# Seven row slots instead of nine, four weight tiles held in their place, and the choice of experts cut into four parts

## The chip, the cores and the metric

The kernel runs on one core of a Trainium2 chip. The core has five engines with a program each: TensorE (PE, with its weight loads as PEld), VectorE (DVE), ScalarE (ACT), GpSimd (POOL) and SyncE (SP), and 16 DMA engines that all transfers share. The metric is the device time of one execution in microseconds (us). Before the change it was 1616.74 us, the median of 3 runs (1616.18 to 1619.26).

## The reference, cut to what matters

Two layers over 256 positions of width 1024. Each has a token mixer (a gated MLP in the first, gated linear attention in the second), then a PEER block. All is float32; every sum below is what the kernel computes.

```
for i in range(2):
    h = rmsnorm(x, norm_mix[i]);  x = x + mixer_a(...) if i == 0 else x + mixer_b(...)
    h = rmsnorm(x, norm_ffn[i]);  x = x + peer(h, ...)
return rmsnorm(x, final_norm)

def peer(h, w_q, k1, k2, u_tab, v_tab):          # per position, 8 heads
    q = h @ w_q                                   # 8 x 256
    s1, s2 = q[:128] . k1, q[128:] . k2           # 128 scores each
    v1, i1 = top_k(s1, 16);  v2, i2 = top_k(s2, 16)
    top_s, pos = top_k(v1 + v2 (all 256 pairs), 16)
    eid  = i1 * 128 + i2 at pos                   # expert numbers, 16 per head
    gate = softmax(top_s)
    act  = gelu(u_tab[eid] . h)                   # 16 dots of length 1024
    return sum over heads and picks of gate * act * v_tab[eid]

mixer_b: proj = h @ w_in; decays, chunked attention; o = rmsnorm(o) * silu(r); return o @ w_out
```

## The kernel before

The 256 positions are two halves (h = 0, 1) of 128, one position per partition. A *row* n is one pick of one head for one half: its GpSimd gather fetches for each of the 128 positions the 2048 numbers (u and v) of that position's expert, 128 x 8 KB = 1.05 MB, into one of 9 row slots (`ROW_SLOTS`, `gather`, L407). There are 2 layers x 2 halves x 8 heads x 16 picks = 512 rows; 16 rows of one head are a *group* j, and k is the row's place in it. Row n passes through every engine:

- VectorE: `dot` (L944) multiplies the u half with hn and sums it, when the gather has landed.
- ScalarE: `gelu` for a pair of rows (L573, `BATCH` = 2), and `weigh` (L587), which makes a diagonal matrix of gate x gelu.
- TensorE: the diagonal times the v half, two products of 512 columns (each two instructions), accumulated in PSUM; it then raises `row_used` (L1399).
- GpSimd: the gather of row n + 9 waits for `row_used` of row n. The first of a group, k = 0, also waits for `ids_ready`, the group's expert numbers.

The numbers of group j come from `choose(j)` on VectorE (L890): two lists of 128 scores cut to 16 each, 112 candidate sums cut to 16, then positions turned into numbers. It stands as one piece behind dot k = 7 of the group before (L1082), for j = 16 and 24 behind k = 1 (`NEXT_CHOICE`). `gates` (L937) stands behind k = 13 and waits for ScalarE's exponentials.

Every engine's order is the order in which its program is written; nothing is reordered. Beside the rows, tables of numbers (`SUMS`, `FIRST_QK`, `FIRST_RV`, `FIRST_BOUT`, `HEAD_PLACES` and so on) say behind which row each step of other work stands: the first layer's queries during rows 0 to 39, the second mixer for half 0 during rows 128 to 255 and for half 1 during rows 256 to 383, the second layer's queries in between and after.

Weights of that other work are tiles of 128 x 1024 (0.5 MB) which SyncE loads through 4 `raw` slots in the order of the list `WEIGHTS` (L102), each when TensorE has used the tile 4 places before (`weight_used`). The second mixer's output weights `b_out`, 8 tiles, stand there twice, once for each half. `block_row` (L1252) uses them.

The row slots are laid over the memory that the first mixer used, the second mixer's tensors (`gq` and so on) behind them.

Of the kernel before, what the change touches and what calls it, by code (L numbers as in the profile page):

```python
# [29 lines left out]
F32 = mybir.dt.float32  # L30
# [7 lines left out]
P = 128  # L38
D = 1024
# [3 lines left out]
TILE = 1024  # L43
# [16 lines left out]
P_HEADS = 8  # L60
P_ROWS = 2 * P_HEADS
NK = 128
TOPK = 16
PICKS = P_HEADS * TOPK
ROWS = TT * PICKS
GROUPS = 2 * TT * P_HEADS
# [8 lines left out]
ROW_SLOTS = 9  # L75
# [16 lines left out]
N_WQ = P_ROWS  # L92
# [10 lines left out]
    [("b_qk", c, 0) for c in range(N_BQK)] + [("b_rv", c, 0) for c in range(N_BRV)] + [("b_out", c, 0) for c in range(N_BOUT)]  # L103
# [4 lines left out]
    + [("b_out", c, 1) for c in range(N_BOUT)] + [("w_q1", c, 1) for c in range(N_WQ)])  # L108
# [9 lines left out]
NEXT_CHOICE = 113  # L118
# [39 lines left out]
def trunk(nc, t, out):  # L158

    with ExitStack() as ctx:  # L160
# [3 lines left out]
        def sem(name):  # L164
            return ctx.enter_context(nc.semaphore(name))
# [9 lines left out]
        def overlay(parts):  # L175
# [46 lines left out]
            ("pad_rows", [P, ROW_SLOTS * 2 * D], F32),  # L222
# [16 lines left out]
        ])  # L239
        ed, qe, ke = [ed0, ed1], [qe0, qe1], [ke0, ke1]  # L240
# [51 lines left out]
        early_loaded = sem("early_loaded")  # L292
# [35 lines left out]
        def _(sp):  # L328
# [4 lines left out]
            def load(src, slot):  # L333
                sp.dma_start(raw[slot][:, :], src).then_inc(raw_loaded[slot], 16)
# [28 lines left out]
            for m, (name, c, h) in enumerate(WEIGHTS):  # L363
                if m < RAW_SLOTS:
                    sp.wait_ge(query_used, N_WQ - RAW_SLOTS + m + 3)
                else:
                    sp.wait_ge(weight_used, m - RAW_SLOTS + 1)
                load(t[name][c], m % RAW_SLOTS)
            for b in range(2 * TT):
                h, cols = b // 2, slice(b % 2 * BANK, b % 2 * BANK + BANK)  # L370
                sp.wait_ge(hn_ready[4], b + 1)
                sp.dma_start(out[h][:, cols], hn[:, h, cols]).then_inc(stored, 16)
# [352 lines left out]
        def _(dve):  # L725
# [18 lines left out]
            def after(number):  # L744
                dve.wait_ge(dve_chain, number)
# [144 lines left out]
            def choose(j):  # L890
# [4 lines left out]
                else:  # L895
# [3 lines left out]
                      [topi[:, h, k, :] for k in range(2)])  # L899
                after(chain[0])  # L900
# [7 lines left out]
                after(d1)  # L908
                top16([cand[:, h, :]], [candv[:, h, :]], [candpos[:, h, :]])
# [16 lines left out]
                after(d2)  # L926
                full = [P, 2, TOPK, TOPK]
# [69 lines left out]
            def mix(h, w):  # L997
# [52 lines left out]
                if w == NEXT_CHOICE:  # L1050
                    choose((2 + h) * P_HEADS)
# [13 lines left out]
            choose(0)  # L1065
            for n in range(2 * ROWS):
                dot(n)
                _, h, g, k = group_of(n)
                w = n % PICKS
                j = n // TOPK + 1  # L1070
                if n == 1:
                    gates(0)
                if PICKS <= n < 3 * PICKS:
                    mix(n // PICKS - 1, w)
                if n >= 3 * PICKS:
                    if w == SUMS:
                        add_sums(4, 0, 4, [(row_used, 3 * PICKS)] * 2)
                    if w == ROOT:
                        add_eps(4, 0)
                    if w == SCALED:  # L1080
                        scale(4, 0, 3)
                if k == TOPK // 2 - 1 and j < GROUPS and j not in (2 * P_HEADS, 3 * P_HEADS):  # L1082
                    choose(j)
                if k == TOPK - 3 and j < GROUPS:
                    gates(j)
# [8 lines left out]
        def _(pe):  # L1094
# [157 lines left out]
            def block_row(name, c, h, a, bank, start, stop):  # L1252

                w = weight(name, c, h)
                for d in range(2):
                    ins = product(psum[:, bank + d, :], a, w[:, d * BANK:(d + 1) * BANK], start=start, stop=stop)
                ins.then_inc(weight_used, 1)
# [207 lines left out]
```

## Time and profile before

| | |
|---|---|
| median of 3 runs | 1616.74 us |
| the profiled execution, its time | 1616.94 us |
| its span | 1614.9 us |
| TensorE busy, share of the span | 1379.0 us, 85% |
| VectorE | 1040.0 us, 64% |
| ScalarE | 661.1 us, 41% |
| GpSimd | 588.6 us, 36% |
| mean granted TensorE clock | 0.952 |
| moved by DMA | 632.15 MB, mean 391 GB/s |

The span is from the first to the last instruction on the core; the time has a little around it. Busy shares of engines overlap, since they work side by side, and are averages over stages that have different limits: the first mixer until about 180 us, the rows afterwards. The granted clock is the share of 2.4 GHz that TensorE got.

### The profile page before, as it was taken

How to read it: one execution, taken by the hardware profiler on the slowest of the kernel's cores; microseconds unless marked ns; L12 is line 12 of the kernel's file. 1: busy time of each engine (PE TensorE's matmuls, PEld its weight loads, DVE VectorE, ACT ScalarE, POOL GpSimd, SP SyncE). 2: the span in 40 equal slices, each digit the busy share in tenths (PEclk: the TensorE clock that was granted, in tenths of full speed). 3: DMA queues.
4: the chain of work that ended last, by engine and by line, in shares of the span. 5: the costliest groups of instructions: out<-in, count | busy, mean ns of one | idle time of the engine just before them, and what ended most of it. 6: DMA issues, size and time to landing. Idle time of an engine off the chain costs nothing. (4 is left out here: it accounts for less than half of the span.)

```text
span 1614.9 us, 15347 instructions
## 1 busy us (share of the span) xinstructions
PE 1379.0 (85%) x4384; PEld 742.2 (46%) x4384; DVE 1040.0 (64%) x2628; ACT 661.1 (41%) x1731; POOL 588.6 (36%) x536
## 2 busy tenths in 40 slices
PE   7998899977777799997968899899988788887776
PEld 6877756522333364443334565345334344443332
DVE  4684566666666666767666655786566566666664
ACT  4653333333333445744333355553343433333333
POOL 0100244443444433334434334243434334444442
PEclk9999999999999899998999999899999999899999
DMA  6855599999999999999999999999999999999997
GB/s 245 298 206 190 214 422 418 423 417 421 419 419 419 409 414 422 421 423 401 424 418 421 421 422 423 409 423 422 421 422 393 422 422 417 422 404 421 416 408 300
DMA packets 99634, 632.15 MB, mean 391 GB/s; under 512 B 11168, under 2 KB 11296, under 8 KB 33504
## 3 DMA queue, kind: packets, MB, share of 16 engines
q0 software_dynamic: 75504, 545.01, 81.7%
q1 hardware_dynamic: 24048, 86.19, 14.0%
q8 instruction: 34, 0.56, 0.1%
q14 instruction: 48, 0.39, 0.1%
HBM read 630.10 MB, written 1.05 MB: 391 GB/s over the span
## 5 line engine op out<-in xcount | busy, mean ns | idle before, releaser
L1096 PE MATMUL psum<-row,diag 128*128 128x512 f32 x2048 | 973.6, 622 | 212.3 <-ACT diag L594 210.9
L415 POOL DMA_INDIRECT row<-in_uv,ids x512 | 576.8, 1127 | 937.3 <-PE psum L1096 721.7
L950 DVE SCALAR_TENSOR_TENSOR row<-row,hn 128x1024 f32<-128x1024 f32 x512 | 617.0, 1224 | 400.9 <-DMA row<-in_uv,ids 393.3
L1096 PEld LDWEIGHTS psum<-row,diag 128*128 128x128 f32 x2048 | 390.0, 198 | 712.9 <-issue 411.7
L576 ACT ACTIVATE acted<-dots 128x2 f32<-128x2 f32 (+1 forms) x257 | 52.1, 203 | 707.5 <-DVE row L950 706.9
L594 ACT ACTIVATE diag<-gate_diag,acted 128x128 f32<-128x128 f32 x512 | 177.9, 387 | 0.2
L585 ACT ACTIVATE gate_diag<-consts,gate 128x128 f32<-128x128 f32 x512 | 173.8, 386 | 0.0
L730 DVE TENSOR_TENSOR tile_lo<-raw,tile_hi 128x1024 fp32r<-128x1024 f32 x48 | 58.7, 1223 | 58.8 <-ACT tile_hi L446 58.8
L1096 PE MATMUL psum<-raw,hT_mix 128*128 128x512 f32 x192 | 90.2, 592 | 0.0
L446 ACT ACTIVATE tile_hi<-raw 128x1024 fp32r<-128x1024 f32 x48 | 50.7, 1058 | 76.7 <-PE psum L1096 72.6
L1096 PEld LDWEIGHTS psum<-hT_query,raw 128*128 128x128 f32 x512 | 63.1, 194 | 15.4 <-issue 15.4
L1096 PE MATMUL psum<-hT_query,raw 128*128 128x128 f32 x512 | 63.0, 277 | 0.0
L1096 PEld LDWEIGHTS psum<-raw,hT_mix 128*128 128x128 f32 x192 | 36.5, 190 | 45.9 <-issue 45.9
L950 DVE DVE_READ_ACCUMULATOR row<-row,hn 128x1 f32 x512 | 42.1, 82 | 0.0
L569 ACT ACT_TABLE_LOAD x32 | 41.1, 1283 | 0.6
L568 ACT ACT_TABLE_LOAD x31 | 39.8, 1283 | 0.6
L940 DVE TENSOR_REDUCE head_sum<-gate 128x1 f32<-128x16 f32 x32 | 5.4, 168 | 46.5 <-ACT gate L568 46.1
L1096 PE MATMUL psum<-tile_hi,hT_hi 128*128 128x512 f32 x128 | 34.7, 393 | 0.5 <-ACT hT_hi L481 0.5
L1096 PE MATMUL psum<-tile_hi,hT_lo 128*128 128x512 f32 x128 | 34.3, 390 | 0.7 <-DVE hT_lo L779 0.7
L1096 PEld LDWEIGHTS psum<-hT_mix,raw 128*128 128x128 f32 x256 | 31.0, 192 | 7.2 <-issue 7.2
L1096 PE MATMUL psum<-tile_lo,hT_hi 128*128 128x512 f32 x128 | 34.2, 389 | 0.0
L576 ACT ACT_TABLE_LOAD x25 | 32.1, 1283 | 0.5
(184 smaller groups left out, 1033.9 us busy)
## 6 DMA issues: line engine op xcount, KB each, us to landing
raw<-in_w_q SPq DMA_DIRECT2D x40, 512.0 KB
raw<-in_a_in SPq DMA_DIRECT2D x32, 512.0 KB
raw<-in_b_rv SPq DMA_DIRECT2D x32, 512.0 KB
raw<-in_a_out SPq DMA_DIRECT2D x16, 512.0 KB
row<-in_uv,ids POOLq DMA_INDIRECT x512
raw<-in_b_qk SPq DMA_DIRECT2D x16, 512.0 KB
raw<-in_b_out SPq DMA_DIRECT2D x16, 512.0 KB
early_q<-in_w_q SPq DMA_DIRECT2D x8, 512.0 KB, 5.8
```

Of the source, the lines that this page charges most:

```text
L415: pool.indirect_dma_start(rows[s][:, :], None, t[f"uv{l}"][:, :], bass.IndirectOffsetOnAxis(ids[:, h, g, k:k + 1], 0)).then_inc(row_loaded ...
L446: act.activation(tile_hi[slot % SPLIT_SLOTS][:, :], raw[slot][:, :], ACT.Copy).then_inc(hi_ready, 1)
L568: act.activation(gate[:, h, g, :], gate[:, h, g, :], ACT.Exp).then_inc(exps, 1)
L569: act.preload_act_table(ACT.Gelu)
L576: act.activation(acted[:, h, g, k:k + many], dots[:, h, g, k:k + many], ACT.Gelu).then_inc(gelu_done, 1)
L585: act.activation(gate_diag[:, n % (2 * BATCH), :], ident, ACT.Copy, scale=gate[:, h, g, k:k + 1]).then_inc(gate_spread, 1)
L594: act.activation(diag[:, n % DIAGS, :], gate_diag[:, n % (2 * BATCH), :], ACT.Copy, scale=acted[:, h, g, k:k + 1]).then_inc(diag_ready, 1)
L730: dve.tensor_tensor(tile_lo[s][:, :], raw[slot][:, :], tile_hi[s][:, :].bitcast(F32), ALU.subtract).then_inc(lo_ready, 1)
L940: after(did(dve.tensor_reduce(head_sum[:, h:h + 1], gate[:, h, g, :], AX.X, ALU.add)))
L950: dve.scalar_tensor_tensor(u, u, 1.0, hn[:, h, :], ALU.mult, ALU.mult, accum_out=dots[:, h, g, k:k + 1]).then_inc(dotted, 1)
L1096: return pe.matmul(o, a, b, start=start, stop=stop, skip_group_check=True)
```

## The change

Three things. `ROW_SLOTS` goes from 9 to 7, and in the memory of the two slots lie four tiles `held0` to `held3`, loaded once with the first four tiles of `b_out` (between the loads of `b_rv` for half 0) and used for both halves; the list `WEIGHTS` has `b_out` from tile 4 on only. `choose` becomes a generator with three stops, so four parts, and one part stands behind each of the dots k = 4 to 7 (behind k = 0 to 3 for j = 16 and 24). `NEXT_CHOICE` goes.

```diff
--- before.py
+++ after.py
@@ -72,7 +72,8 @@
 NARROW = 4
 CANDS = WIDE_ROWS * TOPK + (TOPK - WIDE_ROWS) * NARROW
 
-ROW_SLOTS = 9
+ROW_SLOTS = 7
+HELD = 4
 BATCH = 2
 DIAGS = 8
 FIRST_Q = 6
@@ -100,12 +101,12 @@
 HEADS_AHEAD = 2
 HEADS_EARLY = 6
 WEIGHTS = (
-    [("b_qk", c, 0) for c in range(N_BQK)] + [("b_rv", c, 0) for c in range(N_BRV)] + [("b_out", c, 0) for c in range(N_BOUT)]
+    [("b_qk", c, 0) for c in range(N_BQK)] + [("b_rv", c, 0) for c in range(N_BRV)] + [("b_out", c, 0) for c in range(HELD, N_BOUT)]
     + [("w_q1", c, 0) for c in range(2 * HEADS_EARLY)][:2 * HEADS_AHEAD]
     + [("w_q1", c, 0) for c in range(2 * HEADS_AHEAD, 2 * HEADS_EARLY)]
     + [("b_qk", c, 1) for c in range(N_BQK)] + [("b_rv", c, 1) for c in range(N_BRV)]
     + [("w_q1", c, 0) for c in range(2 * HEADS_EARLY, N_WQ)]
-    + [("b_out", c, 1) for c in range(N_BOUT)] + [("w_q1", c, 1) for c in range(N_WQ)])
+    + [("b_out", c, 1) for c in range(HELD, N_BOUT)] + [("w_q1", c, 1) for c in range(N_WQ)])
 PLACE = {w: m for m, w in enumerate(WEIGHTS)}
 
 
@@ -115,7 +116,7 @@
 FIRST_RV, SIGMOID, SILU = 29, 48, 51
 OUT, O_SCALED, O_TURN, FIRST_BOUT = 65, 73, 73, 77
 X_SUMS, X_ROOT, X_TURN = 95, 97, 100
-NEXT_CHOICE = 113
+FIRST_PART = 4
 HEAD_PLACES = (
     [(0, g, PICKS + 104 + 6 * g) for g in range(2)] + [(0, 2 + i, 2 * PICKS + 3 * i) for i in range(4)]
     + [(0, 6 + i, 2 * PICKS + 62 + 8 * i) for i in range(2)]
@@ -219,7 +220,7 @@
             ("b_in", [P, 2 * A_WIDTH], F32),
         ])
         (_, gq, gk, gcum, ed0, ed1, qe0, qe1, ke0, ke1, k_last, score_in, score_x, bv, br, bo, masks) = overlay([
-            ("pad_rows", [P, ROW_SLOTS * 2 * D], F32),
+            ("pad_rows", [P, 18 * TILE], F32),
             ("gq", [P, B_HEADS, P], F32),
             ("gk", [P, B_HEADS, P], F32),
             ("gcum", [P, B_HEADS, P], F32),
@@ -237,6 +238,7 @@
             ("bo", [P, D], F32),
             ("masks", [P, B_LEVELS + 1, P], U32),
         ])
+        held = overlay([("pad_slots", [P, ROW_SLOTS * 2 * D], F32)] + [(f"held{j}", [P, TILE], F32) for j in range(HELD)])[1:]
         ed, qe, ke = [ed0, ed1], [qe0, qe1], [ke0, ke1]
         z_la, z_tmp = qe0.rearrange("p a b -> p (a b)"), ke0.rearrange("p a b -> p (a b)")
         early_b = overlay([("pad_early", [P, 21 * TILE], F32)] + [(f"early_q{j}", [P, TILE], F32) for j in range(EARLY_Q // 2)])[1:]
@@ -289,7 +291,7 @@
         ain_biased, ain_gelu = sem("ain_biased"), sem("ain_gelu")
         v_meaned, v_squares, v_ms, v_std, v_normed = sem("v_meaned"), sem("v_squares"), sem("v_ms"), sem("v_std"), sem("v_normed")
         sv_done, y_ready, y_turned, yT_hi_ready, yT_lo_ready = sem("sv_done"), sem("y_ready"), sem("y_turned"), sem("yT_hi_ready"), sem("yT_lo_ready")
-        early_loaded = sem("early_loaded")
+        early_loaded, held_loaded = sem("early_loaded"), sem("held_loaded")
         gates_ready, gate_spread, ids_ready, shifted, exps = (
             sem("gates_ready"), sem("gate_spread"), sem("ids_ready"), sem("shifted"), sem("exps"))
         query_used = sem("query_used")
@@ -366,6 +368,8 @@
                 else:
                     sp.wait_ge(weight_used, m - RAW_SLOTS + 1)
                 load(t[name][c], m % RAW_SLOTS)
+                if N_BQK <= m < N_BQK + HELD:
+                    sp.dma_start(held[m - N_BQK][:, :], t["b_out"][m - N_BQK]).then_inc(held_loaded, 16)
             for b in range(2 * TT):
                 h, cols = b // 2, slice(b % 2 * BANK, b % 2 * BANK + BANK)
                 sp.wait_ge(hn_ready[4], b + 1)
@@ -897,6 +901,7 @@
                 after(chain[0])
                 top16([scores[:, h, 2 * g + k, :] for k in range(2)], [topv[:, h, k, :] for k in range(2)],
                       [topi[:, h, k, :] for k in range(2)])
+                yield
                 after(chain[0])
                 for ranks, cols, place in ((slice(0, WIDE_ROWS), slice(0, TOPK), slice(0, WIDE_ROWS * TOPK)),
                                            (slice(WIDE_ROWS, TOPK), slice(0, NARROW), slice(WIDE_ROWS * TOPK, CANDS))):
@@ -906,6 +911,7 @@
                     did(dve.tensor_tensor(cand[:, h, place].rearrange("p (a b) -> p a b", a=m), v1, v2, ALU.add))
                 d1 = did(dve.tensor_copy(topi16[:, h, :, :], topi[:, h, :, :]))
                 after(d1)
+                yield
                 top16([cand[:, h, :]], [candv[:, h, :]], [candpos[:, h, :]])
                 after(chain[0])
                 dve.tensor_tensor(gate[:, h, g, :], candv[:, h, :], candv[:, h, 0:1].broadcast_to([P, TOPK]),
@@ -924,6 +930,7 @@
                 after(d2)
                 d2 = did(dve.tensor_tensor(pos[:, h, 1, :], pos[:, h, 1, :], part2[:, h, :], ALU.add))
                 after(d2)
+                yield
                 full = [P, 2, TOPK, TOPK]
                 d2 = did(dve.tensor_tensor(look[:, 0:2, :, :], pos[:, h, :, :].unsqueeze(3).broadcast_to(full),
                                            iota[:, 0:TOPK].unsqueeze(1).unsqueeze(1).broadcast_to(full), ALU.is_equal))
@@ -1047,8 +1054,6 @@
                     add_eps(3, h)
                 if w == X_TURN:
                     scale(3, h, 2)
-                if w == NEXT_CHOICE:
-                    choose((2 + h) * P_HEADS)
 
             for h in range(TT):
                 add_sums(1, h, 2 * h, [(sums_done, 2 * h + 1), (sums_done, 2 * h + 2)])
@@ -1062,7 +1067,9 @@
                 dve.wait_ge(hn_turned[1], 3 + half)
                 dve.tensor_copy(hT[:, 4 * half:4 * half + 4, P:T],
                                 psum[:, 6 + half, :].rearrange("p (a b) -> p a b", a=4)).then_inc(hT_ready, 1)
-            choose(0)
+            for _ in choose(0):
+                pass
+            choice = iter(())
             for n in range(2 * ROWS):
                 dot(n)
                 _, h, g, k = group_of(n)
@@ -1079,8 +1086,10 @@
                         add_eps(4, 0)
                     if w == SCALED:
                         scale(4, 0, 3)
-                if k == TOPK // 2 - 1 and j < GROUPS and j not in (2 * P_HEADS, 3 * P_HEADS):
-                    choose(j)
+                if j < GROUPS and k == (FIRST_PART if j % P_HEADS or j == P_HEADS else 0):
+                    choice = choose(j)
+                if k < FIRST_PART + 4:
+                    next(choice, None)
                 if k == TOPK - 3 and j < GROUPS:
                     gates(j)
             add_sums(4, 1, 6, [(last_row_half, 1), (row_used, 2 * ROWS)])
@@ -1251,10 +1260,14 @@
 
             def block_row(name, c, h, a, bank, start, stop):
 
-                w = weight(name, c, h)
+                kept = name == "b_out" and c < HELD
+                w = held[c] if kept else weight(name, c, h)
+                if kept:
+                    pe.wait_ge(held_loaded, 16 * HELD)
                 for d in range(2):
                     ins = product(psum[:, bank + d, :], a, w[:, d * BANK:(d + 1) * BANK], start=start, stop=stop)
-                ins.then_inc(weight_used, 1)
+                if not kept:
+                    ins.then_inc(weight_used, 1)
 
             def head_query(h, g, part):
 
```

VectorE's instructions at one choice of the first layer, before: `row,dots` is a dot, `topv` and `topi` are the 16 best of a list of scores and their places, `cand` the 112 sums, `candv` and `candpos` their 16 best.

```order
L950 SCALAR_TENSOR_TENSOR row,dots<-row,hn 128x1024 x10
L876 MAX topv<-scores 128x8 x2
L879 MAX_INDEX topi<-topv,scores 128x8 x2
L882 MATCH_REPLACE scores<-topv,scores 128x128 x2
L885 MAX topv<-scores 128x8 x2
L888 MAX_INDEX topi<-topv,scores 128x8 x2
L906 TENSOR_TENSOR cand<-topv 128x64
L906 TENSOR_TENSOR cand<-topv 128x48
L907 CAST topi<-topi 128x32
L876 MAX candv<-cand 128x8
L879 MAX_INDEX candpos<-candv,cand 128x8
L882 MATCH_REPLACE cand<-candv,cand 128x112
```

The same place in the changed kernel:

```order
L957 SCALAR_TENSOR_TENSOR row,dots<-row,hn 128x1024 x7
L880 MAX topv<-scores 128x8 x2
L883 MAX_INDEX topi<-topv,scores 128x8 x2
L886 MATCH_REPLACE scores<-topv,scores 128x128 x2
L889 MAX topv<-scores 128x8 x2
L892 MAX_INDEX topi<-topv,scores 128x8 x2
L957 SCALAR_TENSOR_TENSOR row,dots<-row,hn 128x1024
L911 TENSOR_TENSOR cand<-topv 128x64
L911 TENSOR_TENSOR cand<-topv 128x48
L912 CAST topi<-topi 128x32
L957 SCALAR_TENSOR_TENSOR row,dots<-row,hn 128x1024
L880 MAX candv<-cand 128x8
```

The choice now begins behind 7 dots of the run, not 10; a dot stands between the scores' best and the sums, and one between the sums and their best.

The end of a choice on VectorE, before (`look` and `numbers` turn positions into expert numbers, `ids`; `head_sum` is the first of the gates):

```order
L925 TENSOR_TENSOR pos<-pos,part 128x16
L928 TENSOR_TENSOR look<-pos,consts 128x512
L931 TENSOR_TENSOR look<-look,topi 128x512
L933 TENSOR_REDUCE numbers<-look 128x32
L935 SCALAR_TENSOR_TENSOR ids<-numbers 128x16
L950 SCALAR_TENSOR_TENSOR row,dots<-row,hn 128x1024 x6
L940 TENSOR_REDUCE head_sum<-gate 128x1
```

And changed:

```order
L931 TENSOR_TENSOR pos<-pos,part 128x16
L957 SCALAR_TENSOR_TENSOR row,dots<-row,hn 128x1024
L935 TENSOR_TENSOR look<-pos,consts 128x512
L938 TENSOR_TENSOR look<-look,topi 128x512
L940 TENSOR_REDUCE numbers<-look 128x32
L942 SCALAR_TENSOR_TENSOR ids<-numbers 128x16
L957 SCALAR_TENSOR_TENSOR row,dots<-row,hn 128x1024 x6
L947 TENSOR_REDUCE head_sum<-gate 128x1
```

A dot stands ahead of the last part too; the six dots between the choice and the gates stay.

SyncE's loads from the second mixer's half 0 on, before (`raw` the four slots that rotate):

```order
L334 DMA raw<-in_b_qk 128x1024 x8
L334 DMA raw<-in_b_rv 128x1024 x16
L334 DMA raw<-in_b_out 128x1024 x8
L334 DMA raw<-in_w_q 128x1024 x12
L334 DMA raw<-in_b_qk 128x1024 x8
L334 DMA raw<-in_b_rv 128x1024 x16
L334 DMA raw<-in_w_q 128x1024 x4
L334 DMA raw<-in_b_out 128x1024 x8
L334 DMA raw<-in_w_q 128x1024 x16
```

And changed, `held` the four tiles that stay:

```order
L336 DMA raw<-in_b_rv 128x1024
L372 DMA held<-in_b_out 128x1024
L336 DMA raw<-in_b_rv 128x1024 x12
L336 DMA raw<-in_b_out 128x1024 x4
L336 DMA raw<-in_w_q 128x1024 x12
L336 DMA raw<-in_b_qk 128x1024 x8
L336 DMA raw<-in_b_rv 128x1024 x16
L336 DMA raw<-in_w_q 128x1024 x4
L336 DMA raw<-in_b_out 128x1024 x4
L336 DMA raw<-in_w_q 128x1024 x16
```

Four loads of `b_out` stand in each half instead of eight; the piece begins just ahead of the fourth held one, and the first three stand in the same way before it.

## Rows read from the trace of the kernel before

**Rows 1.** The page: span, the DMA engines in 40 slices, the gathers' queue.
```profile
span 1614.9 us, 15347 instructions
...
DMA  6855599999999999999999999999999999999997
...
q0 software_dynamic: 75504, 545.01, 81.7%
```

**Rows 2.** Stretches: PE, PEld, DVE, ACT, POOL busy (x count), PEclk, DMA share, GB/s.
```profile
200.00:1600.00 1400.00, 1193.61 (x3519) 592.48 (x3518) 919.36 (x2441) 565.11 (x1595) 573.56 (x513) 0.95 1.01 418
200.00:330.00 130.00, 128.35 (x407) 73.99 (x406) 83.81 (x225) 49.05 (x150) 58.43 (x51) 0.99 1.01 421
380.00:400.00 20.00, 12.16 (x25) 5.21 (x25) 17.05 (x59) 8.27 (x23) 6.93 (x6) 0.83 1.02 421
540.00:1300.00 760.00, 664.81 (x2138) 339.89 (x2136) 502.78 (x1344) 338.80 (x892) 293.98 (x261) 0.96 1.01 418
600.00:740.00 140.00, 126.06 (x367) 61.71 (x365) 96.89 (x252) 74.62 (x167) 53.12 (x47) 0.97 1.02 422
1220.00:1240.00 20.00, 19.15 (x85) 11.58 (x84) 11.88 (x49) 8.00 (x22) 8.52 (x8) 0.98 0.93 363
```

**Rows 3.** Who waited for whom: GpSimd; total us, times, longest.
```profile
POOL row L415 <- PE psum L1096: 721.7, 442, 8.2
POOL row L415 <- DVE ids L935: 193.7, 22, 113.4
```

**Rows 4.** Timeline, two steady rows and a choice: start, duration, engine, line, idle before.
```profile
366.62 1.23 DVE L950 SCALAR_TENSOR_TENSOR row<-row,hn 128x1024 f32<-128x1024 f32 x1 [1.26 <-DMA row<-in_uv,ids]
...
369.12 1.23 DVE L950 SCALAR_TENSOR_TENSOR row<-row,hn 128x1024 f32<-128x1024 f32 x1 [1.26 <-DMA row<-in_uv,ids]
...
371.52 3.70 PE L1096 MATMUL psum<-row,diag 128*128 128x512 f32 x8 [1.29 <-ACT diag L594]
...
373.77 0.94 POOL L415 DMA_INDIRECT row<-in_uv,ids  x1 [2.34 <-PE psum L1096]
...
375.49 0.94 POOL L415 DMA_INDIRECT row<-in_uv,ids  x1 [0.78 <-PE psum L1096]
...
380.19 0.48 DVE L876 MAX8 topv<-scores 128x8 f32<-128x128 f32 x2
...
382.66 0.34 DVE L906 TENSOR_TENSOR cand<-topv 128x64 f32<-128x64 f32 x2
...
383.13 0.28 DVE L876 MAX8 candv<-cand 128x8 f32<-128x112 f32 x1
...
386.18 0.69 DVE L928 TENSOR_TENSOR look<-pos,consts 128x512 bf16<-128x512 bf16 x1
...
388.17 1.22 DVE L950 SCALAR_TENSOR_TENSOR row<-row,hn 128x1024 f32<-128x1024 f32 x1
388.52 1.68 POOL L415 DMA_INDIRECT row<-in_uv,ids  x1 [3.88 <-DVE ids L935]
...
389.31 1.22 DVE L950 SCALAR_TENSOR_TENSOR row<-row,hn 128x1024 f32<-128x1024 f32 x1
...
391.71 8.71 PE L1096 MATMUL psum<-row,diag 128*128 128x512 f32 x16 [6.57 <-ACT diag L594]
```

**Rows 5.** Timeline: the first gather, and the first dot.
```profile
183.96 1.00 POOL L415 DMA_INDIRECT row<-in_uv,ids  x1 [113.41 <-DVE ids L935]
...
190.66 1.23 DVE L950 SCALAR_TENSOR_TENSOR row<-row,hn 128x1024 f32<-128x1024 f32 x1 [7.00 <-DMA row<-in_uv,ids]
```

**Rows 6.** Timeline in the query stage: gather 33 and dot 31, counted from 0.
```profile
268.38 0.96 POOL L415 DMA_INDIRECT row<-in_uv,ids  x1 [2.01 <-PE psum L1096]
...
270.10 1.25 DVE L950 SCALAR_TENSOR_TENSOR row<-row,hn 128x1024 f32<-128x1024 f32 x1
```

**Rows 7.** Timeline beside the second mixer, group 22: a query copy, and its gates.
```profile
1222.80 0.28 ACT L556 ACTIVATE qT<-psum 128x128 f32<-128x128 f32 x1 [3.15 <-PE psum L1096]
...
1228.14 0.17 DVE L940 TENSOR_REDUCE head_sum<-gate 128x1 f32<-128x16 f32 x1 [7.55 <-ACT gate L568]
```

## The prediction

> **What bounds the kernel now.** I read the page first, then stretches, then waits, then the timeline at the places where the change acts. The page shows the 16 DMA engines over 90% busy from the sixth slice to the last but one, and the gathers' queue with 82% of their time [rows 1]. The stretches put a number on it: wherever the queue is full the engines move 422 GB/s, over 600 to 740 us for instance, with TensorE busy 126 of 140 us; over 200 to 1600 us the mean is 418 [rows 2]. So nearly the whole program runs at the rate of the transfers, and what it loses to them is 1400 x (1 - 418/422) = 13.3 us. Of that, 540 to 1300 us (where the second mixer and the second layer's queries run beside the gathers) has 760 x 4/422 = 7.2 us, the query stage 200 to 330 us has 130 x 1/422 = 0.3 us, and the rest, steady gathering, 5.8 us [rows 2]. One execution counts: its time was 1616.9 us for a span of 1614.9, within 0.2 us of the median of the three runs shown.
>
> The losses come in bursts. The clearest is 1220 to 1240 us, 363 GB/s [rows 2]. The waits say what starves the queue: GpSimd waits for TensorE to free a slot (442 times, which costs nothing while the queue is full), and 22 times for expert numbers from VectorE; without the first of 113.4 us that is 80.3 us over 21 times, 3.8 us each [rows 3]. The timeline shows one: the choice holds VectorE from 380.19 to 388.17 us, 7.98 us, and GpSimd, with a free slot, sits 3.88 us until the numbers are there; TensorE then idles 6.57 us and runs its next 16 matmuls in 8.71 us where 8 took 3.70, at a mean clock of 0.83 in that stretch [rows 2, 4].
>
> **Part 1, four tiles held.** Eight loads of b_out for half 0 and eight for half 1 become eight and four: four loads of 128 x 1024 x 4 B = 0.52 MB less, 2.10 MB. At 422 GB/s [rows 2] that is 5.0 us off a queue that sets the time. The held loads move earlier, between loads of b_rv; the engines serve them at the same price, so the move is worth 0, and if they delay gathers then, they free as much time later. The extra wait of TensorE on them is for loads issued some 50 rows earlier: 0.
> The row gives 422 GB/s. The page "DMA: Bandwidth & Descriptors" of the Trainium skill, section "Where 436 GB/s comes from", says that for HBM to SBUF the HBM side (about 358 GB/s per core) binds; by it the 2.10 MB would be worth 5.9 us. This case's trace does not agree, at 422, and I use 422.
>
> **Part 2, the choice in four parts.** It has the same instructions, so VectorE's total stays. From the timeline the parts last 2.47 us (from 380.19 to the sums at 382.66), 0.47 (to 383.13), 3.05 (to 386.18) and 1.99 us (to 388.17) [rows 4]. A dot takes 1.15 us back to back (388.17 to 389.31), a row comes every 2.48 us (366.62 to 369.12) [rows 4]. So behind dot 4 the next starts 1.15 + 2.47 - 2.48 = 1.1 us late, then 0.3 late behind the second part, 0.3 + 1.15 + 3.05 - 2.48 = 2.0 late behind the third, 2.6 behind the fourth, 1.3 a row later, 0 two later. ScalarE takes dots in pairs, so what counts is the odd row of a pair: at most 2.0 us late. Now it is the whole 7.98 us less one row's slack of 1.33, 6.6 us. The wait for expert numbers goes: with seven slots gather 16j waits for row 16j-7, the tenth row of its group, and the numbers are ready after the eighth. What is late next is only the slot.
>
> **Part 3, seven slots.** A slot's round, from rows: from the start of the even dot (366.62) through TensorE (371.52) to the end of the next gather's issue in its slot (373.77 + 0.94) is 8.1 us; for the odd one 376.43 - 369.12 = 7.3 us [rows 4]. From the end of an issue to the dot, with nothing queued ahead, the one observation is the first gather: 190.66 - 184.96 = 5.7 us [rows 5]. Together 13.8 and 13.0 us. Seven slots at 2.48 us give 17.4, spare 3.6 us; nine give 22.4, spare 8.6. Now 6.6 us of lateness, plus the 3.8 us wait, exceeds 8.6 by a little: this is the loss of 5.8 us over some fifteen steady groups, 0.4 each. Afterwards 2.0 of lateness stands against 3.6: no loss. I leave 1 us for it (bounds 0 and 5.8).
> The row says 5.7 us for a gather alone. The same page of the skill, section "Anatomy of one DMA — SWDGE (gpsimd) path", has a fixed 2.0 us and the bytes at 436 GB/s, which for 1.05 MB would be 4.4 us; the spare would be 4.9 us and not 3.6. It leaves the sum as it is.
>
> The price of fewer slots shows where TensorE is the limit. In the query stage it is busy 128.35 of 130 us [rows 2]: it falls behind the gathers row by row, and nine slots let the transfers run on. With two fewer, gather 31 can't be issued before gather 33 is now, at 269.34 us, since it waits for the same row; with 5.7 us its dot starts at 275.0 instead of 270.10 [rows 5, 6]. TensorE's own times don't change there. So the transfers fall 4.9 us behind once, and as they set the time afterwards, that stays: +4.9 (bounds: 0, if they catch up in gaps that I don't see; 5.0, two periods of 2.48, if the rows are used as now).
>
> From 540 to 1300 us a row comes every 760/261 = 2.9 us, since weights take a share [rows 2]; the round is 20.3 us and the spare 6.5, against 12.3 now. Here ScalarE and VectorE also wait in their order behind TensorE's extra work: in group 22 the gates waited 7.55 us, behind query copies that waited 3.15 us for TensorE, which the choice had held back just before [rows 7]. Shorter stops help all of these, the smaller spare hurts. Nothing in the trace has both; bounds are 0 (all recovered) and 7.2 + 16 = 23 us (each of 16 groups 1 us worse than now). I take 5 us, near today's 7.2, since relief and spare both shrink by about 5 us.
>
> **Sum.** 1616.9 - 5.0 (bytes) - 13.3 (all of today's idle) + 4.9 (idle in the query stage) + 1 (in the steady groups) + 5 (beside the mixer) = **1609.5 us**.
>
> **Rivals.**
> 1. *Nearly all idle goes.* The short parts keep TensorE at full clock and the lateness beside the mixer stays under 6.5 us. For: 6.6 us falls to 2.0. Against: the query stage owes nothing to the choice. With 2 us left in all beside the 4.9: 1616.9 - 5.0 - 13.3 + 4.9 + 2 = 1605.5; with half the query price 1603.
> 2. *An even trade.* Every burst of TensorE work costs what the query stage costs: the columns near 580 us and the four heads after 930 us too. For: TensorE is busy 664.81 of 760 us beside the mixer [rows 2]. Against: over 600 to 740 us it had 14 us to spare [rows 2]. Three times 4.9, and 2 of rest: 1616.9 - 5.0 - 13.3 + 14.7 + 2 = 1615.3.
> 3. *Slower: the slots run dry beside the second mixer.* In-order waits like the 7.55 us of the gates [rows 7] stay, since they come from TensorE's queries and not from the choice, and each now exceeds a spare of 6.5 us where it fitted 12.3. For: today's worst loss, 363 GB/s, is at such a wait. Against: the choice stood just ahead of it. The price is 1 us more than now in each of the 16 groups, 23 us in that stretch: 1616.9 - 5.0 - 13.3 + 4.9 + 1 + 23 = 1627.5. It decides from 12.4 us of idle in 540 to 1300 us on, a rate there below 422 x (1 - 12.4/760) = 415 GB/s.
>
> **How the numbers follow.** A measurement of this kernel can't tell less than about 0.2% (3.2 us) from no change. Forecast 0.60, rival 1 0.12, rival 2 0.15, rival 3 0.13. The forecast's own range is 1604 to 1614; rival 1 reaches down to 1601, rival 2 up to 1618, and I go to 1620 to leave out only the most of rival 3. Faster by over 0.2% (under 1613.5): nearly all of the forecast, rival 1 and a bit of rival 2, 0.70. Same: 0.17. Slower: 0.13.
>
> **What would show it.** In the changed profile: b_out is loaded 12 times and 2.1 MB less are moved; GpSimd no longer waits for expert numbers save once at the start; VectorE's stops between dots are at most 3 us; TensorE's clock stays near 1.0 in the steady groups; steady stretches 422 GB/s; the query stage falls from 421 to about 406 GB/s (4.9 of 130 us); 540 to 1300 us stays near 419. The forecast is wrong if the steady groups fall under 420 GB/s (the round is longer than 13.8 us), or the mixer's stretch under 415 (rival 3), or the query stage shows no loss (then 5 us better).

## The result: 0.29% slower

The changed kernel takes 1622.16 us (median of 22 runs, 1615.84 to 1626.45) against 1617.46 us (22 runs) for the kernel before: ratio 1.0029, 95% interval 1.0023 to 1.0036. Forecast were 1609.5 us, 1601 to 1620; the time lies outside the range, on the side to which a chance of 0.13 was given. Below, a difference in us is a difference of ratios times 1617.5 us; it is good to about 1.5 to 3 us.

### The profile page after: what moved, and what is told of

It reads as the page before. It is cut to its first block and busy times, and to the rows that moved or that the text cites. A ratio compares the mean times of both kernels' runs of the same rounds, so it can differ in the third digit from the quotient of the medians.

```text
span 1621.3 us, 15405 instructions
## 1 busy us (share of the span) xinstructions
PE 1391.6 (86%) x4384; PEld 736.8 (45%) x4384; DVE 1039.4 (64%) x2628; ACT 659.7 (41%) x1731; POOL 583.1 (36%) x536
## 3 DMA queue, kind: packets, MB, share of 16 engines
q1 hardware_dynamic: 23472, 84.09, 13.6%
## 5 line engine op out<-in xcount | busy, mean ns | idle before, releaser
L957 DVE SCALAR_TENSOR_TENSOR row<-row,hn 128x1024 f32<-128x1024 f32 x512 | 624.0, 1224 | 473.5 <-DMA row<-in_uv,ids 462.6
L419 POOL DMA_INDIRECT row<-in_uv,ids x512 | 571.3, 1116 | 953.5 <-PE psum L1105 814.2
L1105 PEld LDWEIGHTS psum<-row,diag 128*128 128x128 f32 x2048 | 382.7, 197 | 724.9 <-issue 388.7
L1105 PE MATMUL psum<-raw,hT_mix 128*128 128x512 f32 x160 | 75.2, 592 | 0.0
L1105 PEld LDWEIGHTS psum<-raw,hT_mix 128*128 128x128 f32 x160 | 30.4, 190 | 38.3 <-issue 38.3
L957 DVE DVE_READ_ACCUMULATOR row<-row,hn 128x1 f32 x512 | 41.9, 82 | 0.0
L572 ACT ACT_TABLE_LOAD x31 | 39.8, 1283 | 0.5
L1105 PE MATMUL psum<-hT_mix,raw 128*128 128x128 f32 x256 | 31.2, 275 | 0.0
```

Of the source, the lines that this page charges most:

```text
L419: pool.indirect_dma_start(rows[s][:, :], None, t[f"uv{l}"][:, :], bass.IndirectOffsetOnAxis(ids[:, h, g, k:k + 1], 0)).then_inc(row_loaded ...
L572: act.activation(gate[:, h, g, :], gate[:, h, g, :], ACT.Exp).then_inc(exps, 1)
L957: dve.scalar_tensor_tensor(u, u, 1.0, hn[:, h, :], ALU.mult, ALU.mult, accum_out=dots[:, h, g, k:k + 1]).then_inc(dotted, 1)
L1105: return pe.matmul(o, a, b, start=start, stop=stop, skip_group_check=True)
```

## The profile after

The page of the changed kernel, to set beside [rows 1]: span, the DMA engines' busy share and rate in 40 slices, and the two large queues.

```profile
span 1621.3 us, 15405 instructions
...
DMA  6855599999999999999999999999999999999997
GB/s 240 301 199 194 221 373 383 424 416 405 419 422 421 394 423 422 422 416 418 421 405 423 421 423 405 423 417 407 415 417 403 422 422 418 423 419 413 420 421 295
...
q0 software_dynamic: 75504, 545.01, 81.6%
q1 hardware_dynamic: 23472, 84.09, 13.6%
```

Its stretches (columns as in [rows 2]):

```profile
200.00:1600.00 1400.00, 1199.11 (x3508) 583.73 (x3507) 915.58 (x2436) 562.31 (x1590) 568.28 (x514) 0.97 1.01 415
200.00:330.00 130.00, 125.02 (x393) 71.85 (x392) 79.72 (x219) 45.46 (x140) 54.99 (x48) 0.97 0.99 395
540.00:1300.00 760.00, 670.95 (x2135) 339.42 (x2136) 503.88 (x1347) 343.67 (x901) 288.50 (x262) 0.97 1.01 415
600.00:740.00 140.00, 125.54 (x368) 62.27 (x367) 91.50 (x219) 71.03 (x161) 45.44 (x44) 0.96 1.01 420
1220.00:1240.00 20.00, 19.15 (x84) 11.37 (x83) 9.61 (x29) 8.04 (x23) 9.87 (x9) 1.00 1.00 406
```

The bytes came out as forecast: the page's q1 has 84.09 MB, against 86.19 before. The worst hole, 363 GB/s over 1220 to 1240 us, is at 406, but the 20 us ahead of it are at 385 where they were at 423: over 1200 to 1240 us it has moved and hardly shrunk (393 before, 396 now). And the query stage, 200 to 330 us, moves 395 GB/s and not the 406 forecast, and TensorE is busy 125.02 us of it where it was 128.35 [rows 2]: it has to wait for rows there, which is new.

The waits of GpSimd and VectorE in the changed kernel (total us, times, longest):

```profile
POOL row L419 <- PE psum L1105: 814.2, 450, 9.0
DVE row L957 <- DMA row<-in_uv,ids: 462.6, 336, 6.4
POOL row L419 <- DVE ids L942: 113.6, 1, 113.6
DVE head_sum L947 <- ACT gate L572: 10.0, 5, 3.2
```

GpSimd's waits for expert numbers are gone but for the start (22 in [rows 3]); the gates' waits, 7.55 us in [rows 7], are at most 3.2. Every wait that was to go has gone, and the time went up.

The timeline of the changed kernel in a steady group shows the four parts and what they do to a slot (dots at L957, GpSimd's issues at L419):

```profile
420.98 3.70 PE L1105 MATMUL psum<-row,diag 128*128 128x512 f32 x8 [1.26 <-ACT diag L598]
421.06 1.23 DVE L957 SCALAR_TENSOR_TENSOR row<-row,hn 128x1024 f32<-128x1024 f32 x1 [1.24 <-DMA row<-in_uv,ids]
...
424.56 1.21 DVE L957 SCALAR_TENSOR_TENSOR row<-row,hn 128x1024 f32<-128x1024 f32 x1
424.96 1.62 POOL L419 DMA_INDIRECT row<-in_uv,ids  x1 [0.78 <-PE psum L1105]
...
426.16 1.23 DVE L957 SCALAR_TENSOR_TENSOR row<-row,hn 128x1024 f32<-128x1024 f32 x1
...
426.94 5.40 PE L1105 MATMUL psum<-row,diag 128*128 128x512 f32 x8 [2.26 <-ACT diag L598]
...
430.35 1.22 DVE L957 SCALAR_TENSOR_TENSOR row<-row,hn 128x1024 f32<-128x1024 f32 x1
430.90 1.48 POOL L419 DMA_INDIRECT row<-in_uv,ids  x1 [4.32 <-PE psum L1105]
...
433.49 1.22 DVE L957 SCALAR_TENSOR_TENSOR row<-row,hn 128x1024 f32<-128x1024 f32 x1
...
434.63 1.22 DVE L957 SCALAR_TENSOR_TENSOR row<-row,hn 128x1024 f32<-128x1024 f32 x1
...
438.45 1.23 DVE L957 SCALAR_TENSOR_TENSOR row<-row,hn 128x1024 f32<-128x1024 f32 x1 [1.25 <-DMA row<-in_uv,ids]
```

With a row each 2.48 us from 421.06 on, the dots start 1.0, 0.1, 1.9, 2.5 and 1.2 us late: the forecast was 1.1, 0.3, 2.0, 2.6 and 1.3. What was not forecast stands at 426.94: TensorE had idled 2.26 us, its clock fell (below), and the pair of rows took 5.40 us where 3.70 is usual. The issue of the next gather into the slot of the dot at 421.06 ends at 432.38, 11.3 us later, not 8.1. Even so its row is used at 438.45, 17.39 us after 421.06, which is seven rows' time: this round just closes.

And the query stage, gather 31 and dot 31 of the changed kernel, to set beside [rows 6]:

```profile
269.89 0.94 POOL L419 DMA_INDIRECT row<-in_uv,ids  x1 [4.37 <-PE psum L1105]
...
277.10 1.23 DVE L957 SCALAR_TENSOR_TENSOR row<-row,hn 128x1024 f32<-128x1024 f32 x1 [2.23 <-DMA row<-in_uv,ids]
```

Forecast were 269.34 us for the end of the issue and 275.0 for the dot; they are 270.83 and 277.10, since TensorE's own times slipped by 1.5 us and the gather needed 6.3 us and not 5.7.

## The experiments

| kernel | slots, tiles held, choice | ratio to before, 95% | us |
|---|---|---|---|
| e1_nine_split | 9, 0, four parts | 0.9998 [0.9989, 1.0007] | -0.3 |
| e4_eight_split | 8, 2, four parts | 1.0006 [0.9997, 1.0015] | +1.0 |
| e3_seven_split_noheld | 7, 0, four parts | 1.0061 [1.0047, 1.0075] | +9.9 |
| changed kernel | 7, 4, four parts | 1.0029 [1.0023, 1.0036] | +4.7 |
| e2_seven_whole | 7, 4, one piece | 1.0500 [1.0475, 1.0524] | +81 |
| e7_nine_no_choice | 9, 0, none | 0.9964 [0.9950, 0.9978] | -5.8 |
| e13_floor | 9, 0, none; half of row products | 0.9960 [0.9947, 0.9974] | -6.5 |
| e9_seven_no_choice | 7, 4, none | 0.9970 [0.9959, 0.9981] | -4.9 |
| e15_nine_other_rows | 9, 0, one piece | 1.0013 [1.0004, 1.0022] | +2.1 |
| e16_seven_other_rows | 7, 4, four parts | 1.0038 [1.0025, 1.0052] | +6.1 |
| e5_seven_spread | 7, 4, four parts | 1.0012 [1.0002, 1.0022] | +1.9 |
| e6_nine_spread | 9, 0, one piece | 1.0004 [0.9995, 1.0012] | +0.6 |
| e14_nine_spaced | 9, 0, parts two rows apart | 1.0002 [0.9993, 1.0011] | +0.3 |
| e11_seven_spaced | 7, 4, parts two rows apart | 1.0006 [0.9997, 1.0015] | +1.0 |
| e10_nine_seven_nine | 9, 7, 9; 4; four parts | 0.9985 [0.9976, 0.9994] | -2.4 |
| e12_nine_seven_nine_spaced | the same, two rows apart | 0.9974 [0.9965, 0.9984] | -4.2 |

e7, e9 and e13 leave work out and fetch other rows, e15 and e16 only fetch other rows: these five measure times and don't compute the reference's result.

### The change taken apart

```
e1: ROW_SLOTS = 9, HELD = 0        e3: HELD = 0        e4: ROW_SLOTS = 8, HELD = 2
e2:  if j < GROUPS and k == (7 if j % P_HEADS or j == P_HEADS else 1):
         for _ in choose(j): pass
```

> Nine slots, the choice in four parts, all b_out tiles loaded twice: the split alone. Theory (the missing slots cost the time): with nine slots the lateness of some 2 us behind the parts stands against a spare of 8.6 us, the wait for expert numbers stays but only for the last row of the choice, and the idle of 13.3 us falls to about 4: 1608 us, 0.994 of before. Rival (the parts themselves cost, four stops instead of one): not faster than before, 1617 or more.

> Seven slots, four held tiles, the choice in one piece as before: the changed kernel without the split. Theory: lateness of 6.6 us against a spare of 3.6 us costs some 3 us in each of 30 groups, beside the 8 us of the query stage, so 1690 us or more. Rival (parts cost, slots do not): 1622 or less.

> Seven slots and the split, but all b_out tiles loaded twice: the changed kernel without the held tiles. Theory (bytes at 422 GB/s, still on the path): 5 us more than the changed kernel, 1627. Rival (in a kernel with idle gaps the four loads fall into them): the same as the changed kernel, 1622.

> Eight slots, two held tiles, the split. Theory (each slot is one more period of spare, 2.5 us): the query stage loses about 4 us instead of 8, the rest about 4 instead of 16, bytes give 2.5: 1610, faster than before by 0.4%. Rival (slots do not matter, the parts do): 1620 to 1624.

Taken one after the other, the three parts of the change are: the split alone -0.3 us (e1, where some 9 us less were expected), two slots fewer +10.2 (e1 to e3), four tiles held -5.2 (e3 to the changed kernel, forecast -5.0). The split is worth 76 us with seven slots and nothing with nine. The prediction takes out 13.3 us of idle and adds 4.9 + 1 + 5 = 10.9 for what stands with seven slots; measured are 0.3 and 10.2. One slot (e4, two tiles held, taken as worth 2.6) costs 3.9 us; 1610 us was expected of e4 and it took 1.0 us more than the kernel before.

Where the time goes is told by the rows. The table has how many us later than in the kernel before the dot of a row starts, each kernel from its one profiled execution (one execution can lie 3 us off its kernel's median, as e1's does, so go by changes along a line). Rows 0 to 63 hold the query stage, 64 to 127 are steady gathering, 128 to 383 stand beside the second mixer.

| kernel | row 0 | 64 | 128 | 256 | 384 | 511 |
|---|---|---|---|---|---|---|
| before, start in us | 190.7 | 358.9 | 522.2 | 890.8 | 1273.7 | 1604.4 |
| e1 (9 slots, parts) | 1.7 | 1.7 | 2.1 | 1.5 | 2.1 | 3.2 |
| e14 (9, spaced parts) | 0.1 | -0.5 | -0.6 | -1.3 | -0.9 | -0.2 |
| e7 (9, no choice) | -0.3 | 1.3 | 0.3 | -2.1 | -3.7 | -4.7 |
| e13 (9, no choice, less TensorE) | -0.5 | -1.0 | -1.0 | -3.5 | -5.1 | -6.1 |
| changed kernel | 0.3 | 7.9 | 9.1 | 9.9 | 7.1 | 6.4 |
| e3 (7, none held) | 0.6 | 9.2 | 11.4 | 11.4 | 13.2 | 12.4 |
| e11 (7, spaced parts) | 0.2 | 6.7 | 5.3 | 5.6 | 0.9 | 1.9 |
| e9 (7, no choice) | 0.8 | 6.6 | 6.2 | 4.1 | -1.4 | -2.3 |
| e5 (7, queries spread) | -0.8 | 2.0 | 3.7 | 5.5 | 3.3 | 2.8 |
| e2 (7, one piece) | 0.3 | 14.8 | 26.9 | 52.2 | 60.2 | 81.2 |

Seven slots lose most in the query stage (8 to 9 us in the changed kernel and e3), 1 to 2 in the steady rows 64 to 127, about 2 to 3 beside the mixer (the tiles' 5.2 us taken out), and nothing in rows 384 to 511. In e2 a steady group loses some 3 us, as expected there. Between rows 128 and 192 the changed kernel, e9 and e10 fall 5.5 to 5.7 us behind, while e1, e3 and e7, which hold no tiles, stay within 0.5; at row 256 all three have that back. The held loads, 2.10 MB moved forward, cost their time then and free it later, as the prediction says.

### How much idle time there was

```
e7, e9, in choose(j):
+ if j not in (0, P_HEADS):
+     dve.wait_ge(ids_ready, j)
+     dve.tensor_tensor(gate[:, h, g, :], candv[:, h, :], candv[:, h, 0:1].broadcast_to([P, TOPK]), ALU.subtract).then_inc(shifted, 1)
+     dve.tensor_scalar(ids[:, h, g, :], ids[:, h, 0, :], j, None, ALU.bitwise_xor).then_inc(ids_ready, 1)
+     return
e13: e7, and   for d in range(2 if w in (0, PICKS - 1) else 1):   for the row products
e15, e16: the whole choice, only its last instruction replaced by the bitwise_xor
```

> The kernel before without nearly all of the choice: only heads 0 and 8 of the first layer choose; every other group takes the expert numbers of the first head of its half, with its own number put over them bit by bit (so the rows fetched differ), and the gates' sums from that head. VectorE's stop of 8 us goes at each of 30 groups, and GpSimd's wait for numbers with it. The prediction's theory (the 13.3 us between 418 and 422 GB/s are idle time which the choice causes and which can be had back): 1604 to 1607 us. Rival (the DMA engines don't advance alike; a row is there when the slowest is done, and the gaps are those of the faster ones, which had run ahead): 1613 to 1617 us.

> The changed kernel without the choice, in the same way (seven slots, four tiles held). The prediction's theory: 1604 + 4.9 (query stage) - 5 = 1604 us. Rival of the slowest engine: only the steps that seven slots and the burst cost are left; the lateness behind the parts goes: 1611 to 1616 us, and the query stage still shows under 405 GB/s. If it shows 415 or more, the loss there was the parts' and not the burst's.

> The kernel with nine slots and no choice, and of each row's two products on TensorE the second is left out too, save for the first and last row of a half: about 0.93 us of TensorE a row less, so neither VectorE nor TensorE can keep the gathers back. It measures the floor that the transfers set. Theory (1612.6 without the choice is this floor but for 1 or 2 us; the transfers themselves take the rest): 1609 to 1613 us. Rival (the prediction's: 422 GB/s can be held throughout, 1617.5 - 13.3): 1604 us or less; the 8 us that are still there are then waits for TensorE.

> The kernel before with the whole choice carried out, but its last instruction replaced as in the kernels without the choice: the expert numbers used are those of the first head of the half with the group's number put over them, so the same rows are fetched as there. It tells whether the 5.8 us which came back without the choice (0.9964) were the choice's work or the other rows' places in memory. If the choice's work: within 1.5 us of the kernel before, 1616 to 1619 us. If the rows' places: 1611 to 1613 us, and the floor for the real rows lies 5 us higher than the one measured.

> The changed kernel with the same replacement. If the choice's work in parts costs the 9.6 us that lie between 1.0029 and 0.9970: 1621 to 1623 us. If the rows' places make 5 us of it: 1616 to 1618 us, and the parts with seven slots cost only 4 to 5 us.

Without the choice and with TensorE's row work nearly halved, nine slots gain 6.5 us. That is what these causes held back, not 13.3 (more than nine slots were not tried), and e15 and e16 show that it isn't due to the other rows fetched: with them and the full choice both kernels are no faster. (e13 and e7 agree within 0.7 us, so without the choice TensorE's load keeps nothing back.) Where the other 7 us are, two 20 us stretches near the end of e13 show:

```profile
1560.00:1580.00 20.00, 10.94 (x16) 3.36 (x16) 9.87 (x16) 5.67 (x22) 9.76 (x9) 0.83 1.01 421
1580.00:1600.00 20.00, 13.07 (x17) 4.53 (x18) 9.87 (x16) 6.21 (x23) 1.45 (x2) 0.67 0.50 208
```

VectorE's 16 instructions are eight dots in both: rows keep coming every 2.5 us while the rate falls from 421 to 208 GB/s and the engines' busy share to 0.50. The last gather was issued at 1582.27 us: half of the transfer capacity has nothing left to do, and the rest sets the pace. Each gather raises its semaphore 16 times as it lands. These 16 completion marks say the same: from the first to the last lie on average 1.8 us in group 0 and 2.3 to 5.8 from group 8 on in the kernel before, 9 to 11 from group 16 on in e13. So some DMA engines run ahead and others lag, and a row is there when the last has delivered. I take it that a hole in the mean rate can be an engine that has run ahead and waits for new gathers while the slowest works on; no view here tells the engines apart. The kernel before has such a hole near its end, and its rows hardly slow down in it:

```profile
1560.00:1580.00 20.00, 20.00 (x45) 8.72 (x44) 10.35 (x20) 8.14 (x23) 12.69 (x11) 0.94 1.00 394
```

```profile
1562.03 1.23 DVE L950 SCALAR_TENSOR_TENSOR row<-row,hn 128x1024 f32<-128x1024 f32 x1
...
1579.62 1.23 DVE L950 SCALAR_TENSOR_TENSOR row<-row,hn 128x1024 f32<-128x1024 f32 x1 [1.25 <-DMA row<-in_uv,ids]
```

Seven rows take 17.6 us there, 0.2 more than at 2.48 us each, where the prediction's reckoning would count 20 x (1 - 394/422) = 1.3 us. The last dots of two groups, in the kernel before and in e13, show that the choice costs the steady groups nothing:

```profile
1524.71 1.22 DVE L950 SCALAR_TENSOR_TENSOR row<-row,hn 128x1024 f32<-128x1024 f32 x1 [1.24 <-DMA row<-in_uv,ids]
...
1564.51 1.23 DVE L950 SCALAR_TENSOR_TENSOR row<-row,hn 128x1024 f32<-128x1024 f32 x1 [1.24 <-DMA row<-in_uv,ids]
```

```profile
1518.24 1.23 DVE L956 SCALAR_TENSOR_TENSOR row<-row,hn 128x1024 f32<-128x1024 f32 x1 [1.26 <-DMA row<-in_uv,ids]
...
1558.66 1.23 DVE L956 SCALAR_TENSOR_TENSOR row<-row,hn 128x1024 f32<-128x1024 f32 x1 [1.30 <-DMA row<-in_uv,ids]
```

Sixteen rows take 39.8 us before and 40.4 in e13. Why the choice still costs some 6 us with nine slots, whole, split or spaced (e14), isn't settled. Where it does is plainer: up to row 128 e7 is no faster than the kernel before, and of the 4.4 us that it gains from row 0 on it gains 4.0 between rows 128 and 384, beside the second mixer.

### The query stage

```
e5, e6: QUERY_ROWS = 6 (was 4);  the six small loads at n == 5 * TOPK (was 4 * TOPK)
```

> The changed kernel with one query tile every six rows in place of four, so that the ten tiles of the query stage take 60 rows and not 40 (and six small loads behind them are moved from row 64 to row 80). Theory (the burst of TensorE work is what seven slots can't bridge: 395 GB/s over 200 to 330 us, 8.3 us of transfers): a row then leaves TensorE 0.63 us of slack each 2.5 us, about a query's 3.7 us per six rows, and 6 to 8 us come back: 1614 to 1616 us. Rival (seven slots are too few behind every choice, wherever it stands): the time lost moves with the rows and comes out within 2 us of the changed kernel's 1622.

> The kernel before (nine slots, the choice in one piece) with the same spreading of the query tiles. Theory: nine slots bridge the burst already (421 GB/s over 200 to 330 us), so nothing comes back: 1616 to 1619 us. Rival (TensorE's load is what holds every version back): 1611 us or less.

The stretch 200 to 330 us of e5, then of e3 and of e9:

```profile
200.00:330.00 130.00, 120.24 (x360) 65.23 (x359) 83.59 (x227) 46.06 (x144) 55.57 (x51) 0.99 1.00 410
```

```profile
200.00:330.00 130.00, 125.98 (x394) 72.46 (x393) 79.21 (x219) 45.46 (x140) 52.52 (x48) 0.97 1.00 395
```

```profile
200.00:330.00 130.00, 126.78 (x396) 72.85 (x394) 59.98 (x109) 46.19 (x144) 57.71 (x49) 0.97 0.99 400
```

Spread over 60 rows the burst costs seven slots less (410 GB/s for 395), but of the 6 to 8 us expected 2.7 came back: both sides of the expectation missed. In the profiles e5 is 5.9 us ahead of the changed kernel at row 64 and 3.6 at row 511, so the expected gain was there and part of it was lost further on; why wasn't tried. Without the choice the stage shows 400 GB/s against 415 in e7, 130 x 15/422 = 4.6 us: the forecast's 4.9, as long as no part stands in the way.

### The place of the parts

```
- if j < GROUPS and k == (FIRST_PART if j % P_HEADS or j == P_HEADS else 0):
+ if j < GROUPS and k == 1:
      choice = choose(j)
- if k < FIRST_PART + 4:
+ if k % 2 == 1 and k <= 7:
      next(choice, None)
```

> The changed kernel with the four parts two rows apart, behind rows 1, 3, 5 and 7 of every group, in place of one row apart. Theory (the 8 us that the choice still costs with seven slots, 1622.2 against 1614.1 without it, are the lateness that adds up over parts behind one another, up to 2.6 us and a TensorE at half clock, against 3.6 us to spare): with a row between the parts it stays under 1.8 us, and 4 to 8 us come back: 1614 to 1618 us. Rival (it is the parts' mere work and not its place): 1621 us or more.

> Nine slots, none held, and the parts two rows apart: what the best form of the choice brings by itself. Removing it altogether gave 5.0 us (1612.6 against 1617.6), one part behind another nothing. If the place of the parts is what matters: 1613 to 1615 us. If nine slots cover the lateness either way: 1616 to 1618 us, as with the parts one row apart.

A row between the parts brings 3.7 us with seven slots (good to 2 us) and nothing with nine. The same 6 us, 426 to 432 us, in the changed kernel and in e11 (the column ahead of the last two is TensorE's clock):

```profile
426.00:432.00 6.00, 5.06 (x8) 2.08 (x8) 5.62 (x23) 1.57 (x7) 1.68 (x2) 0.72 1.02 423
```

```profile
426.00:432.00 6.00, 4.36 (x10) 1.44 (x8) 5.49 (x11) 1.50 (x7) 3.20 (x3) 1.00 1.02 425
```

Part of these 6 us the changed kernel's TensorE works at the lower of its two levels (1.2 GHz; a mean of 0.72 of 2.4), e11's at the higher throughout; over the span the profiles have 0.97 and 0.99. But this group loses no time by it. Its first dot and the next group's, in the changed kernel and in e11:

```profile
411.12 1.23 DVE L957 SCALAR_TENSOR_TENSOR row<-row,hn 128x1024 f32<-128x1024 f32 x1 [1.25 <-DMA row<-in_uv,ids]
...
450.86 1.22 DVE L957 SCALAR_TENSOR_TENSOR row<-row,hn 128x1024 f32<-128x1024 f32 x1 [1.25 <-DMA row<-in_uv,ids]
```

```profile
408.17 1.23 DVE L957 SCALAR_TENSOR_TENSOR row<-row,hn 128x1024 f32<-128x1024 f32 x1 [1.25 <-DMA row<-in_uv,ids]
...
447.96 1.23 DVE L957 SCALAR_TENSOR_TENSOR row<-row,hn 128x1024 f32<-128x1024 f32 x1 [1.25 <-DMA row<-in_uv,ids]
```

Sixteen rows take 39.7 and 39.8 us. With seven slots and no choice at all the two slots cost 1.0 + 5.2 = 6.2 us (e7 to e9, the held tiles' gain taken out); with adjoining parts 10.2; so adjoining parts add 4.0, and spacing them gives back 3.7. By the rows, e11 is 1.2 us ahead of the changed kernel at row 64, 3.8 at row 128 and 4.5 at row 511. That the place of the parts matters is shown; by which step they cost, the clock or the lateness itself, is not.

### A version that beats both

```
+ ROW_SLOTS, FEWER, NARROWED, WIDENED = 9, 7, 142, 350
+ def slots():                 # for each row: its slot, the row that used it last, its turn
+     for n in range(2 * ROWS):
+         free = range(FEWER if NARROWED <= n < WIDENED else ROW_SLOTS)
+         s = min(free, key=lambda s: last.get(s, (s - 100, 0))[0])
...
+         if s >= FEWER and n >= WIDENED:
+             before = max(before, WIDENED - 10)
```

> The changed kernel (parts, four tiles held), but rows use nine slots up to row 141 and from row 350 on, and seven only between, while the held tiles lie in the room of the other two. Theory (the seven slots cost 4.4 to 8 us in the query stage, before row 48, and little beside the mixer, where the held tiles save 5.2): 1617.3 (nine slots, parts, none held) - 5.2 + 1 to 2 = 1613 to 1614 us, and the query stage is back at 421 GB/s. Rival 3 of the prediction (the slots run dry beside the mixer): 1618 us or more.

> Both: nine, seven and nine slots, and the parts two rows apart. If the lateness behind parts costs something beside the mixer, 1611 to 1613 us; if not, within 1 us of the same kernel with the parts one row apart.

The held tiles are needed from about row 150 to row 339 only. With nine slots outside that, the query stage of e10 is full again:

```profile
200.00:330.00 130.00, 127.90 (x406) 73.80 (x406) 84.79 (x232) 48.95 (x150) 54.74 (x51) 0.99 1.01 422
```

e10 is 7.1 us faster than the changed kernel, 2.4 faster than the one before; with the parts spaced, e12, 1613.7 us, 0.26% faster than before (0.9974, 0.9965 to 0.9984). The intervals of e10 and e12 overlap, so what spacing adds here isn't shown. e12 is the only version below the kernel before by more than 0.2% with all the work in it. With seven slots in rows 142 to 349 alone, 2.1 us (e1 to e10) of the 5.2 us of the tiles are left, so the slots cost 3 us there and not the 16 that rival 3 adds to today's idle.

## Why the prediction was wrong

- **"- 5.0 (bytes)"**: right, 5.2 us.
- **"- 13.3 (all of today's idle)": the step that failed**, in size and in cause. I took 422 GB/s, the rate of the fullest stretches, as one that the whole program can hold, and read each hole in the mean as time lost. The split took the waits for expert numbers away and brought 0.3 us with nine slots (e1), nothing when spaced (e14). The whole forecast was -7.4 us and the time went up by 4.7, a miss of 12.1; this term alone is off by 13.0. With the holes' supposed causes taken out altogether only 6.5 us came back (e13). The "loss of 5.8 us over some fifteen steady groups" wasn't there: rows 64 to 127 come as fast with the whole choice as without it (e7, e13), since nine slots cover its stop. What the choice does cost stands beside the mixer, and cutting it into parts doesn't give it back.
- **"+ 4.9 (idle in the query stage)"**: right mechanism, too small. 4.6 us without the choice, 130 x (1 - 395/422) = 8.3 with it (7.9 us late at row 64): with the parts in place TensorE's own times slipped, by 1.5 us at gather 31, which "TensorE's own times don't change there" denied.
- **"+ 1 (in the steady groups)"**: about right. The parts' lateness was right to 0.2 us. The round was not: I held TensorE's clock near 1.0, but an idle time of 2.26 us was followed by the lower level, the pair took 5.40 us, and from dot to the end of the issue were 11.3 us. With the 6.1 us that this gather needed (432.38 to 438.45) that is just the 17.4 that seven slots have, a spare of nothing where I had left 1.6 (3.6 less 2.0). The changed kernel loses 1.2 us in rows 64 to 127 and none in rows 384 to 511.
- **"+ 5 (beside the mixer)"**: in the profiles 415 GB/s for 418, 760 x 3/422 = 5 us more, of which part is again only the mean. e10, with seven slots only there, is 2.1 us better than e1, so the slots cost 3 us there beside a gain of 5.2.
- **Waits for expert numbers**: gone as forecast, and worth nothing with nine slots. With seven, one piece costs 76 us more, so the split is what makes seven slots possible, not a gain by itself.
- **Rivals**: the time lies between rival 2 (1615.3) and rival 3 (1627.5), and neither is what happened. Of rival 2's bursts only the query stage leaves a lasting loss: between rows 128 and 192 (about 530 to 730 us) the held loads take their 5 us and give them back, and from row 256 on the changed kernel falls no further behind. Rival 3 adds 16 us to today's idle beside the mixer; the slots cost 3 there. Both had the gain of 13.3 in their sums. Had it been 0, the forecast's own sum would have been 1622.8, near the 1622.2 measured. That the 10.9 us of the other terms match the 10.2 that two slots cost is partly luck: the query stage took more than its 4.9, and the 5 beside the mixer stood for idle time that stays, not for a price of the slots.

## What to carry to other kernels

A dip in the mean transfer rate is lost time only if the slowest engine dips too: look at whether the consumer's rows slow down in it, and measure the floor by leaving work out before counting on the difference. Buffers are priced at the bursts, and a room needed for part of a program can be given back outside it. On a ring with little to spare try a unit of work between short stops: with seven slots it brought 3.7 us, with nine nothing.

## What was unexpected of the hardware

- A gather's 16 completion marks drift apart, from 1.8 us in group 0 of the kernel before to 11 us in e13 and 12.3 in e14, whose time is the same as before; in the changed kernel, whose queue is shorter, they stay within 4.4 on average. Rows came at the same pace at 208 and at 421 GB/s.
- GpSimd's issue of a gather took at most 1.00 us where VectorE ran nothing in its first 0.94 us (79 of the 512 in the kernel before, 142 in e13), and up to 1.99 us where a dot ran beside it, with a choice near or not: at 435.00 us in the changed kernel, beside a dot and after the choice's end, 1.66 us. e13, without the choice, has the longer mean (1.153 us, 1.127 before) and is the faster kernel, so this isn't what the choice costs.
- TensorE at a mean clock of 0.83 over 200 to 1600 us in e13 lost nothing, since it had time to spare; with seven slots a pair at the lower level used up the spare time of its slot, and still no row came late for it.
- The changed kernel's times scatter over 10.6 us (22 runs), those of the kernel before over 3.7 (22 runs), those of e11 over 4.1 (11 runs). Why wasn't tried.
